# Four tiles side by side at the start of each large stage of a hybrid decoder layer, with other banks and another place for the sums of squares

## The reference

```python
x = x + 0.5 * rmsnorm(swiglu(rmsnorm(x, g1), w_gate, w_up, w_down), g1_post)   # D_FF = 5632
proj = rmsnorm(x, g_mix_pre) @ w_in        # q, k, v, o: 1024 columns each; glu a, b: 1024 each; i, f gates: 4 each
hm = sigmoid(o) * mlstm_chunkwise(q, k, v, i, logsigmoid(f), C0, n0, m0)        # 4 heads of 256
hc = silu(layernorm(depthwise_conv31(a * sigmoid(b))))
x = x + rmsnorm(concat(hm, hc) @ w_out, g_mix_post)
x = x + 0.5 * rmsnorm(swiglu(rmsnorm(x, g2), w2_gate, w2_up, w2_down), g2_post)
```

## Time and profile before

| | |
|---|---|
| median of 3 runs | 2265.08 us (2263.3 to 2266.26) |
| the profiled execution: time, span | 2256.01 us, 2254.3 us |
| mean granted clock of TensorE, as a share of 2.4 GHz | 0.991 |
| TensorE busy (matmuls), share of the span | 2200.4 us, 98% |
| VectorE, ScalarE, GpSimd busy | 997.6, 894.0, 1094.9 us |
| HBM read, written | 357.06 MB, 13.07 MB |

### The profile page before, as it was taken

One profiled execution on the slowest core, in us unless ns is written; L12 is line 12 of the kernel. 1 busy time (PEld: TensorE's weight loads), 2 busy tenths in 40 slices (PEclk: granted clock), 3 DMA queues, 4 the chain that ended last, 5 costly groups with the idle time before them and its releaser, 6 DMA issues. The chain is left out here.

```text
span 2254.3 us, 42520 instructions
## 1 busy us (share of the span) xinstructions
PE 2200.4 (98%) x16484; PEld 2177.2 (97%) x16484; DVE 997.6 (44%) x1327; ACT 894.0 (40%) x1138; POOL 1094.9 (49%) x633
## 2 busy tenths in 40 slices
PE   8999999999999998999999998999999999999995
PEld 8999999999999997999999997999999999999995
DVE  7434432233333226867757716544442223333324
ACT  5433333333333335434344535434343333333331
POOL 5444443344444445646657576444443334444444
PEclk9999999999999999999999999999999999999998
DMA  5555555545455542555645452554555545454542
GB/s 188 184 165 170 161 175 164 163 158 167 167 161 166 168 165 83 202 187 182 227 154 204 150 176 93 170 171 163 169 164 170 165 159 167 167 163 158 168 165 88
DMA packets 100309, 371.15 MB, mean 165 GB/s; under 512 B 11120, under 2 KB 13296, under 8 KB 99216
## 3 DMA queue, kind: packets, MB, share of 16 engines
q1 hardware_dynamic: 96192, 349.93, 46.8%
q10 hardware_dynamic: 3920, 20.18, 2.5%
q0 software_dynamic: 128, 0.07, 0.0%
HBM read 357.06 MB, written 13.07 MB: 164 GB/s over the span
## 5 line engine op out<-in xcount | busy, mean ns | idle before, releaser
L1453 POOL TENSOR_TENSOR wlo<-raw,whi 128x1024 fp32r<-128x1024 f32 x367 | 894.1, 2438 | 810.1 <-ACT whi L725 797.0
L367 PE MATMUL bank<-xh,whi 128*128 128x288 f32 x3600 | 1076.1, 299 | 18.3 <-DVE xl L1031 14.9
L368 PE MATMUL bank<-xl,whi 128*128 128x288 f32 x3600 | 1063.7, 295 | 0.0
L369 PE MATMUL bank<-xh,wlo 128*128 128x288 f32 x3600 | 1061.2, 295 | 0.0
L725 ACT ACTIVATE whi<-raw 128x1024 fp32r<-128x1024 f32 x658 | 693.3, 1056 | 640.6 <-PE bank L369 623.8
L1014 DVE TENSOR_TENSOR wlo<-raw,whi 128x1024 fp32r<-128x1024 f32 x291 | 438.4, 1506 | 773.6 <-ACT whi L725 773.6
L367 PEld LDWEIGHTS bank<-xh,whi 128*128 128x128 f32 x3600 | 680.3, 189 | 30.4 <-DVE xl L1031 15.3
L368 PEld LDWEIGHTS bank<-xl,whi 128*128 128x128 f32 x3600 | 681.1, 189 | 0.8
L369 PEld LDWEIGHTS bank<-xh,wlo 128*128 128x128 f32 x3600 | 679.4, 189 | 0.0
L369 PE MATMUL bank<-hh,wlo 128*128 128x288 f32 x1408 | 417.5, 296 | 0.0
L367 PE MATMUL bank<-hh,whi 128*128 128x288 f32 x1408 | 416.1, 296 | 0.0
(11 more groups left out here) (213 smaller groups left out, 1181.9 us busy)
## 6 DMA issues: line engine op xcount, KB each, us to landing
raw<-stream SPq DMA_DIRECT2D x658, 512.0 KB, 3.4
C<-c_in ACTq DMA_DIRECT2D x4, 2048.0 KB, 8.0
cs_out<-C ACTq DMA_DIRECT2D x4, 2048.0 KB, 8.1
x_res<-x_in SPq DMA_DIRECT2D x4, 576.0 KB, 9.8
y_out<-x_res SPq DMA_DIRECT2D x3, 576.0 KB, 2.9
conv_out<-upad ACTq DMA_DIRECT2D x4, 302.0 KB, 4.2
upad<-conv_in ACTq DMA_DIRECT2D x4, 272.0 KB, 3.2
cp_out<-cpr ACTq DMA_DIRECT2D x4, 256.0 KB, 9.6
```

What stands on the lines that cost most here:

```text
L367: pe.matmul(out, wh, mov_hi[:, k, :], start=first, stop=False)
L368: pe.matmul(out, wh, mov_lo[:, k, :], start=False, stop=False)
L369: return pe.matmul(out, wl, mov_hi[:, k, :], start=False, stop=last)
L1453: pool.tensor_tensor(wlo[:, g % SLOTS, :], raw[:, g % SLOTS, :], whi[:, g % SLOTS, :].bitcast(F32), ALU.subtract).then_inc(lo_ready[g % SL ...
```

## The change

- **Four tiles side by side.** `project_first` takes the place of `project_two` and of the gates' own tile: the first four tiles (`FIRST = 4`; in the mixer the gates and the head's first three conv tiles) are multiplied chunk by chunk, 12 matmuls a chunk, 16 chunks. The weights are laid out in that order, so a piece holds two chunks of four tiles.
- **Splits among the chunks.** Pieces 4 to 9 are now split, hi and low, before chunks 6, 8, 10, 12, 14 and 15 in `residual` and 8, 10, 12, 14, 15, 15 at the first start, in the queues of all three engines.
- **Sums of squares.** The mixer's squares are summed by VectorE's tree as in the feed-forward stages, and one column sum replaces the 16. All three column sums stand in the middle of the fifth tile (mixer: at the end of piece 6).
- **Spare banks.** The fifth and sixth tile of a feed-forward stage, and in the mixer the gates' tile and k0 of head 0, use banks 5 and 6, and need not wait for an eviction.
- **Evictions.** The first four tiles are evicted together once rstd is there; in the feed-forward stages eight tiles, not four, are now written out ahead of the loop.
- **Gates.** Their rows move from `scr` to a buffer of their own (`gt`); a0, b0, a1 and b1 of head 0 are evicted between the steps of the gates' chain; the broadcasts of every head come two pieces later (k = 6), as do what hangs on them (k = 7, 8, 9, 10 for 5, 6, 7, 8), head 0's taps three pieces later, and its memory query, attention and updates three pieces later (`LATE`). `DVE_LO` loses 5, 7, 9, 20, 21, 22, 28, 29 and gets 26, 28 and 31.

The core of the diff:

```diff
-START_SPLITS = {0: 0, 1: 1, 2: 4, 3: 5, 4: 13}
-NEXT_SPLITS = {4: 11}
+START_SPLITS = {0: 0, 1: 1, 2: 3, 3: 5, 4: 8, 5: 10, 6: 12, 7: 14, 8: 15, 9: 15}
+NEXT_SPLITS = {4: 6, 5: 8, 6: 10, 7: 12, 8: 14, 9: 15}
+FIRST = 4
...
-TAPS_FROM = 10
-DVE_LO = {h + k for h in KEYS_AT[:3] for k in (12, 13, 14, 20, 21)} | {5, 7, 9}
+TAPS_FROM = (13, 10, 10, 10)
+LATE = (3, 0, 0, 3)
+MIX_FROM = (FIRST - 1) * XC // CH
+DVE_LO = {h + k for h in KEYS_AT[1:3] for k in (12, 13, 14, 20, 21)} | {h + k for h in KEYS_AT[:1] for k in (18, 20, 23)}
...
+SPARE_BANK = {4: 5, 5: 6, GATE_T: 5, tile_of(0, "k0"): 6, FFN2_T + 4: 5, FFN2_T + 5: 6}
...
+            def project_first(T, g, x_from):
+                for t in range(FIRST):
+                    tile_start(T + t, 0, None)
+                for f in range(FIRST * XC):
+                    k, t = divmod(f, FIRST)
+                    n, j = divmod(f, CH)
+                    if j == 0:
+                        piece_start(g + n, 0, None)
+                    if t == 0:
                         pe.wait_ge(x_ready, x_from + k + 1)
+                    last = multiply(T + t, g + n, j, k, xh, xl, k == 0, k == XC - 1)
+                    if j == CH - 1:
+                        last.then_inc(piece_done, 1)
...
+                        def square_sum(k):
+                            if k == CH - 1:
+                                pe.wait_ge(xsq_sum, sums)
+                                column_sums(bank[4][:, 0:TOK], y[:, 0, :])
+
+                        project_first(T, g, x_from)
+                        for q in range(FIRST, 2 * FIRST):
+                            project(T + q, g + 2 * q, 0, 0, None, square_sum if q == FIRST else None)
+                        start = 2
...
             pe.wait_ge(norm_var, 2)
-            project(GATE_T, GATE_P, 0, 0, None, XC, between=lambda k: k and square_sum(k - 1))
-            square_sum(XC - 1)
+            project_first(GATE_T, GATE_P, XC)
...
-                    if (k, j) == (4, 2):
+                    if (k, j) == (6, 2):
                         broadcast_rows(h)
...
+                if (p, j) == (MIX_FROM, CH - 1):
+                    pe.wait_ge(xsq_sum, 2)
+                    column_sums(bank[4][:, 0:TOK], y[:, 0, :])
...
             def residual(g, post, pre, n_x, n_new):
 
                 for c in range(XC + 1):
                     if c < XC:
+                        for p in NEXT_SPLITS:
+                            if NEXT_SPLITS[p] == c:
+                                split_lo(g + p)
                         dve.wait_ge(t_ready, n_new + c + 1)
...
-            def residual(k, n_new):
+            def residual(g, k, n_new):
 
                 pool.wait_ge(rpost_ready, k + 1)
                 for c in range(XC):
+                    for p in NEXT_SPLITS:
+                        if NEXT_SPLITS[p] == c:
+                            split_lo(g + p)
                     times_rpost(n_new, c)
```

More of the change, by code:

```diff
@@ L633, in between @@
                     ln_squares()
-            for p in range(MIX):
+            for p in range(MIX_FROM, MIX):
                 T, g = HEAD_T + p // 2, HEAD_P + p
@@ L748, in ffn @@
                 for half, n in enumerate(FF_HALVES):
-                    def body(i, first):
-                        for jj in range(2):
[L751 to L771, removed]
-                            act.activation(hh[:, jj if i is None else i * 2 + jj, :], scr[:, 4, :], ACT.Copy)\
-                               .then_inc(h_hi, 1)
@@ L775, in ffn, with gate_up @@
-                    if half == 0:
-                        body(None, True)
-                    with act.Fori(1 - half, n // 2) as i:
-                        body(i, False)
+                    def gate_up(i, T, f, k, before, after):
+                        for p in before:
+                            split_hi(p, 8, i)
+                        act.wait_ge(tile_evicted, at(T + 1, 4, i))
+                        if i is not None or f >= 1:
+                            act.wait_ge(gated, at(f, 2, i))
+                        act.activation(scr[:, 2, :], scr[:, f % 2, :], ACT.Sigmoid).then_inc(sig_ready, 1)
+                        for p in after:
+                            split_hi(p, 8, i)
+                        act.wait_ge(h_f32, at(f + 1, 2, i))
+                        act.activation(hh[:, k, :], scr[:, 4, :], ACT.Copy).then_inc(h_hi, 1)
@@ L1407, in ln_part @@
                                       xh[:, 4 * n:4 * n + 4, :].bitcast(F32), ALU.subtract).then_inc(conv_ready, 1)
-            for p in range(1, MIX + 8):
-                if p % 2 == 0 and p <= MIX:
+            for p in range(MIX_FROM, MIX + 8):
+                if p % 2 == 0 and 8 < p <= MIX:
                     evict(p)
@@ L1657, in _pieces, with _order @@
     return np.ascontiguousarray(out.transpose(0, 2, 1, 3)).reshape(len(flat), P, PIECE)
+def _order(tiles, first):
+    return [(t, k) for k in range(XC) for t in tiles[:first]] + [(t, k) for t in tiles[first:] for k in range(XC)]
 def _ffn_pieces(gate, up, down):
@@ L1700 @@
         _ffn_pieces(a["w_ffn1_gate"][0], a["w_ffn1_up"][0], a["w_ffn1_down"][0])
-        + [_pieces(gates, [(0, k) for k in range(XC)]),
-           _pieces(w_in[:, :6 * D_MLSTM], [(t, k) for t in tiles for k in range(XC)]),
+        + [_pieces(np.concatenate([gates, w_in[:, :6 * D_MLSTM]], axis=1), _order([0] + [t + 1 for t in tiles], FIRST)),
            _pieces(a["w_out"][0], out_order)]
```

310 lines of the change are left out of this document (147 added, 163 removed).

## The result

The changed kernel took 2271.31 us (median of 7 runs, 2270.86 to 2275.13), the kernel before 2265.67 us (7 runs): ratio 1.0031, 95% interval 1.002 to 1.0043. Timed once more it took 2276.03 us against 2262.28: ratio 1.0051, interval 1.0035 to 1.0066. It is slower, by 5.6 us in one comparison and 13.8 in the other, that is 0.3 to 0.5%, and both intervals lie clear of 1. The prediction was 2274 us.

The account below looks back on a forecast made before the run. TensorE, busy 98%, was taken as the bound, the three openings losing 39 us. Terms -4.6 + 3.3 + 4.2 + 2.5 - 1.5 + 1.0 + 4.2 = +9.1 took 2256.01 to 2265; with 9 for the median, 2274 us, range 2257 to 2282.

Parts of the forecast that it names:

- The operand chain: Mixer's and second feed-forward stage's openings: splits queued among the chunks delay x and idle TensorE; +3.3 and +4.2 us.
- The wait at 916.33: TensorE's 1.28 us idle in the mixer would be given back: -1.5 us with its restart.
- The first stage: First feed-forward stage's opening, x from DMA: column sum done at 41.5 against 46.04, -4.6 us (bounds -7 and -3).
- The broadcasts: Head 0, piece 14: TensorE would wait there for the gates' rows; +2.5 us (bounds 0.5 and 4.6).
- the gates' rows: Mixer: the later column sum delays rstd and the gates' chain; rows ready 27.5 to 31.5 us behind the eighth piece's end.
- Head 0's backlog: Head 0's taps start later and its memory query three pieces later: +1.0 us (bounds 0 and 3).
- The pitch: Loop behind the second stage's opening: weight matmuls 2.2 ns slower, +4.2 us; first stage's loop 0; together bounds 0 and 8.4.
- the mixer's opening: Eight pieces end at 911.3 against 908.5: +3.3 us (bounds +1 and +5).
- The 9 us between profile and median: Whole kernel: median 2265.08 against profiled 2256.01 us; the difference was added to the forecast 2265, giving 2274.
- Rival 2: Openings: splits don't lock queues, only VectorE's and GpSimd's turns count; mixer and second stage -9 each, 2243 to 2245; chance 0.15.

## Why the prediction was right, and where not

- **The operand chain** held step by step. GpSimd's product 8 was forecast behind the low split of piece 5, and stands there. TensorE stood idle for 4 us ahead of chunk 7 and of chunk 11 and for 3.5 ahead of chunk 14, the chunks that were forecast. The eight pieces end at 912.86, forecast 911.3 from a start 0.5 us earlier. In the second stage they took 43.9 us for the forecast 43. Moving GpSimd's three splits and nothing else gave 10.8 us back per opening: the cause is shown, not only argued. The wait at 916.33 is gone, as forecast.
- **The first stage**: eight pieces end at 39.14 (forecast 39.3), and the sum waits 1.68 us (1.7). The gain is 2.9 in the traces and 3.8 timed, not 4.6: the pieces took 29.7 us, not 29.0 (they started 0.9 us earlier), and the eight pieces behind took 28.3 us where they had taken 25.2: 2.2 for the sum and its wait, 0.2 for slower matmuls right behind it (0.62 us for the first three, 44.54 to 45.16, not 0.4), and the rest for the slower pitch and a slow moment at 54 us.
- **The broadcasts**: the wait is 2.56 us, forecast 2.5. The term was mis-sized all the same, since TensorE's clock fell behind it: the stretch cost 4.2 to 7.3 us more than before. The prediction had priced just such half-clock starts in the openings and left this one out.
- **Why the gates' rows are so late**: three of VectorE's small operations, on 4 partitions, took 2.4 us each beside GpSimd's splits; one of the same size between them, that ran alone, took 0.28. Rows ready 29.9 us behind the eighth piece's end, within the forecast 27.5 to 31.5. The timeline of VectorE and GpSimd:

```profile
931.01 2.50 POOL L1465 TENSOR_TENSOR wlo<-raw,whi 128x1024 fp32r<-128x1024 f32 x1 [1.05 <-ACT whi L735]
931.27 2.38 DVE L1227 COPY lfb<-gt 4x256 f32<-4x256 f32 x1
...
933.58 0.28 DVE L1228 COPY lfm<-gt 4x256 f32<-4x256 f32 x1
```

  The copy that starts 0.26 us behind the split ends 0.14 us behind it. The Trainium skill, page "SBUF — State Buffer", section "SBUF: two separate sides", has VectorE, in a two-port mode or with two inputs in SBUF, and GpSimd share a pair of ports under an exclusive lock, one blocked until the other's instruction is over; these rows agree, though they don't name the copy's mode. The kernel before has the same (a copy of 2.51 us at 898.78, beside a split), so this is no cost of the change.
- **Head 0's backlog** (+1.0): nothing in the traces beyond the 1.5 us of a half-clock stretch, which profiles of either kernel have or lack.
- **The pitch** (+4.2): the step that failed. The prediction took the pitch of a profile for a property of the kernel, with a cause in what stood ahead of the loop. The profile of before was one of the rare executions with both loops fast, 9.1 us under the median of the three runs timed with it; the 4.2 us has no place in the sum. Without it the sum is 4.9 us, for 9.4 to 11.6 measured at equal pitch; the clock at the broadcasts (2 to 5 us more than forecast), the mixer's opening (1 more) and the first stage (1.7 less gained) make the rest. That the total of 9.1 us came so near is luck: the false 4.2 us stood in for what the other terms lacked. That 2274 lies between the two timed medians owes as much to it. The 9 us between profile and median, put on top as a constant, was for 8.5 us this same draw.
- **Rival 2** (only turns count) was false for this change. Once the splits' places no longer tied the queues it was nearly true: from the first product (860.81) to the end of xl 15 (896.06) 35.2 us for its 33, and the eight pieces in 33.1 us for its 31 (868.4 to 899).

## What to carry to other kernels

When work is inserted into several in-order queues "before chunk n", count each queue's own lead: GpSimd ran four chunks ahead of VectorE, so the same n came too early there, and cost 10.8 us per opening. Price a wait of TensorE with the clock behind it. Take a second profile of the same kernel before reading an effect of 0.2% from two traces, and compare stretches, not totals.

## What was unexpected in the hardware

- Two loops of 1920 weight matmuls each took 251.73 or 256.00 us, drawn per execution, at a granted clock of 1.00 either way; a third loop of that length (pieces 144 to 224) always took 256.00. The cause is open.
- A stretch of 3.4 us at half clock is there in some executions of a kernel and missing in others, and costs 1.5 us: pieces 278 to 280 of the kernel before in 9.3 or 10.8 us, with no wait ahead in either. A wait of 0.6 to 3.1 us at the same place was followed by 6.8 or 10.2 us at half clock in all six profiles that had one.
- Taking 29 matmuls out of a stretch that waits for operands left its length at 40.1 us; its mean clock was 0.74, for 0.91 and 0.96 in the two profiles with them.
